# Where VectorE subtracts the transposed attention weights within a step, and where it splits the next weight tile

## The reference, cut to what matters

```python
z = jnp.einsum('bhqd,bhkd->bhqk', qb, kb).astype(jnp.float32) * scale
mask = s_idx < t_idx
log_one_minus = jnp.where(mask, jax.nn.log_sigmoid(-z), 0.0)
suffix = lax.cumsum(log_one_minus, axis=3, reverse=True) - log_one_minus
weights = jnp.where(mask, jnp.exp(jax.nn.log_sigmoid(z) + suffix), 0.0)
outs.append(jnp.einsum('bhqk,bhkd->bhqd', weights.astype(vb.dtype), vb))
...
y_sb = jnp.einsum('bsw,wd->bsd', (o_sb * jax.nn.silu(sb_z)).astype(x.dtype), w_o_sb[layer])
```

## Time and profile before

| | us |
|---|---|
| median of 3 runs | 809.22 |
| the profiled execution | 809.52 |
| its span, first to last instruction | 807.8 |
| TensorE matmuls busy in the span | 791.0 |
| TensorE weight loads busy | 662.3 |
| VectorE busy | 581.6 |
| ScalarE busy | 410.0 |
| granted TensorE clock | 0.999 of full speed |

### The profile page before, as it was taken

How to read it: one execution, slowest core, us unless ns; L and a number is a source line. 1 busy time by engine, 2 the same in 40 slices (tenths; PEclk the granted TensorE clock), 3 DMA queues, 4 the chain that set the end, 5 groups by cost and what they waited for, 6 DMA issues and landing times.

```text
span 807.8 us, 11845 instructions
## 1 busy us (share of the span) xinstructions
PE 791.0 (98%) x4441; PEld 662.3 (82%) x4441; DVE 581.6 (72%) x823; ACT 410.0 (51%) x706; POOL 30.4 (4%) x32
## 2 busy tenths in 40 slices
PE   5999999999999999999999999999999999999996
PEld 4778888888888888889889888888888888888885
DVE  6528997989798798956645646566457777779985
ACT  7526675666666466655244144244343343365442
POOL 1540000000000000020000000000000000000000
PEclk9999999999999999999999999999999999999999
DMA  9862112202120220021111010244443333395222
GB/s 316 277 225 53 27 28 52 52 26 52 53 51 26 53 52 27 27 80 54 30 50 27 3 52 27 79 143 152 147 131 105 105 104 105 105 360 213 105 105 104
DMA packets 72483, 76.31 MB, mean 94 GB/s; under 512 B 3804, under 2 KB 57207, under 8 KB 71928
## 3 DMA queue, kind: packets, MB, share of 16 engines
q1 hardware_dynamic: 72386, 75.71, 29.5%
q10 hardware_dynamic: 54, 0.01, 0.0%
HBM read 55.79 MB, written 15.73 MB: 89 GB/s over the span
## 4 chain that ended last, share of the span: by engine, by line
PE 94%; ACT 2%; DVE 1%; DMA 1%; issue 1%; SPq 0%; DVEq 0%; ACTq 0%
PE pj L698 29%; PE tr L1002 5%; PE sc L950 5%; PE ob L950 5%; PE ob L790 5%; PE pj L842 4%; PE ob L1002 4%; PE pj L1002 4%; PE tr L800 4%; PE sc L1002 3%; PE pj L714 3%; PE pj L823 3%; PE tr L1060 2%; PE sc L767 2%; PE sc L766 2%; PE pj L1060 2%
## 5 line engine op out<-in xcount | busy, mean ns | idle before, releaser
L698 PE MATMUL pj<-h_hi,w_lo 128*128 128x512 f32 x336 | 134.2, 399 | 0.0
L698 PE MATMUL pj<-h_hi,w_hi 128*128 128x512 f32 x336 | 133.9, 398 | 0.0
L698 PE MATMUL pj<-h_lo,w_hi 128*128 128x512 f32 x336 | 133.8, 398 | 0.0
L1671 DVE TENSOR_TENSOR_SCAN surv<-surv 128x128 f32<-128x128 f32 (+3 forms) x64 | 86.5, 1351 | 16.3 <-ACT beta L1169 15.9
L698 PEld LDWEIGHTS pj<-h_hi,w_lo 128*128 128x128 f32 x336 | 63.5, 189 | 12.1 <-issue 0.5
L698 PEld LDWEIGHTS pj<-h_lo,w_hi 128*128 128x128 f32 x336 | 63.3, 189 | 12.0 <-issue 0.3
L698 PEld LDWEIGHTS pj<-h_hi,w_hi 128*128 128x128 f32 x336 | 63.6, 189 | 11.6 <-issue 0.2
L1210 ACT ACTIVATE wt_hi<-tr 128x512 fp32r<-128x512 f32 (+2 forms) x96 | 43.6, 490 | 37.8 <-PE tr L800 36.3
L1594 DVE TENSOR_TENSOR w_lo<-w_raw,w_hi 128x1024 fp32r<-128x1024 f32 x33 | 40.3, 1222 | 27.0 <-ACT w_hi L1102 26.7
L1703 DVE TENSOR_TENSOR wt_lo<-tr,wt_hi 128x512 fp32r<-128x512 f32 (+2 forms) x96 | 50.2, 550 | 7.9 <-ACT wt_hi L1210 7.4
L1674 DVE TENSOR_TENSOR beta<-beta,surv 128x128 f32<-128x128 f32 (+3 forms) x64 | 48.6, 759 | 2.2
(11 more groups left out here) (400 smaller groups left out, 1910.3 us busy)
## 6 DMA issues: line engine op xcount, KB each, us to landing
w_raw<-in_w_in SPq DMA_DIRECT2D x30, 512.0 KB, 3.8
y_scratch<-y_ring SPq DMA_DIRECT2D x28, 256.0 KB, 2.0
graw<-in_w_in SPq DMA_DIRECT2D x14, 512.0 KB, 5.2
y_back<-y_scratch SPq DMA_DIRECT2D x14, 512.0 KB, 5.2
x_t<-in_x SPq DMA_DIRECT2D x8, 512.0 KB, 6.6
wrow<-in_w_out SPq DMA_DIRECT2D x4, 1024.0 KB, 7.2
w_scratch<-wsum SPq DMA_DIRECT2D x4, 1024.0 KB, 5.0
wout_raw<-in_w_out SPq DMA_DIRECT2D x8, 512.0 KB, 7.2
```

Of the source, the lines that this page charges most:

```text
L698: mm = pe.matmul(pj[bank][:, :], (w_lo if p == 2 else w_hi)[:, slot, k, :], (h_lo if p == 1 else h_hi)[:, k, HALF * h:HALF * h + HALF], st ...
L1671: dve.tensor_tensor_scan(s[:, ::-1], s[:, ::-1], s[:, ::-1], 1.0, ALU.mult, ALU.bypass)\
```

## The change

Three statements of the VectorE list of a step trade places; no instruction is added, removed or altered, and no other engine's list changes.

```diff
@@ -1690,20 +1690,12 @@
                         if k < KT - 1 or p < 2:
                             continue
                         c = 8 * i + 6 + 2 * j + h
+                        if h == 0:
+                            low_part(4 * i + 4 + j, j % 2)
                         if j == 0:
                             dve.wait_ge(proj_act, c + 1)
                             dve.tensor_tensor(z_silu[:, HALF * h:HALF * h + HALF], pj[h][:, :], z_sig[:, :],
                                               ALU.mult).then_inc(proj_free, 1)
-                    for n, r in enumerate(ROUNDS):
-                        if r[0] == "w" and r[1] == step:
...
-                            dve.wait_ge(tr_act, RPP * i + R0 + n + 1)
-                            dve.tensor_tensor(wt_lo[g % 2][:, b0:b0 + nb, qs],
...
                     if step >= 3 and step % 2:
...
-                    for j, h, k, p in plan[step]:
-                        if (h, k, p) == (0, KT - 1, 2):
-                            low_part(4 * i + 4 + j, j % 2)
+                    for n, r in enumerate(ROUNDS):
+                        if r[0] == "w" and r[1] == step:
...
+                            dve.wait_ge(tr_act, RPP * i + R0 + n + 1)
+                            dve.tensor_tensor(wt_lo[g % 2][:, b0:b0 + nb, qs],
```

More of the change, by code:

```diff
@@ L1696, in pair @@
                                               ALU.mult).then_inc(proj_free, 1)
-                    for n, r in enumerate(ROUNDS):
-                        if r[0] == "w" and r[1] == step:
-                            unit, b0, nb = r[2:]
-                            g = unit % 8 // 2
-                            qs = slice(P * (unit % 2), P * (unit % 2) + P)
-                            dve.wait_ge(tr_act, RPP * i + R0 + n + 1)
-                            dve.tensor_tensor(wt_lo[g % 2][:, b0:b0 + nb, qs],
-                                              tr[n % 2][:, 0:P * nb].rearrange("p (b q) -> p b q", q=P),
-                                              wt_hi[g % 2][:, b0:b0 + nb, qs].bitcast(F32),
-                                              ALU.subtract).then_inc(tr_free, 1)
                     if step >= 3 and step % 2:
@@ L1717, in pair @@
                                           low, z_silu[own, 256 * g:256 * g + 256], ALU.mult).then_inc(g_done, 1)
-                    for j, h, k, p in plan[step]:
-                        if (h, k, p) == (0, KT - 1, 2):
-                            low_part(4 * i + 4 + j, j % 2)
+                    for n, r in enumerate(ROUNDS):
+                        if r[0] == "w" and r[1] == step:
+                            unit, b0, nb = r[2:]
+                            g = unit % 8 // 2
+                            qs = slice(P * (unit % 2), P * (unit % 2) + P)
+                            dve.wait_ge(tr_act, RPP * i + R0 + n + 1)
+                            dve.tensor_tensor(wt_lo[g % 2][:, b0:b0 + nb, qs],
+                                              tr[n % 2][:, 0:P * nb].rearrange("p (b q) -> p b q", q=P),
+                                              wt_hi[g % 2][:, b0:b0 + nb, qs].bitcast(F32),
+                                              ALU.subtract).then_inc(tr_free, 1)
             with dve.Fori(0, PAIRS - 1) as i:
```

## The result

The changed kernel takes 814.26 us (median of 4, 813.72 to 814.44) against 809.37 of the kernel before: ratio 1.0064, 95% interval 1.0052 to 1.0077. It is slower by 4.9 us; the forecast was 814.3, in a range of 811.9 to 817.0. In a second comparison it was 814.44 against 809.31, ratio 1.0068 (1.0055 to 1.0082).

A forecast was written before the change was run, and what follows sets the result against it. TensorE was taken as the bound, its matmuls busy 791.0 of 807.8 us. +1.31 us in each of the first three pairs (3.9) and 1.0 in the last make +4.9: forecast 814.3 us, range 811.9 to 817.0.

The forecast's parts named there:

- Who waits for `wt_lo`: Second pair: TensorE's AV products and transpositions wait for the delayed `wt_lo`; VectorE's sum of work per step stays the same.
- five partial sums: TensorE's lateness: 0.4 us at AV(7), 0.89 at step 9's scores, 0.69 after AV(9), 0.38 after AV(13), 1.31 behind T(16).
- The loss at AV(7): Step 7: AV(7) reads the later `wt_lo`(6) and loses some 0.4 us, not added because the next wait swallows it.
- What is won back at AV(9) and AV(13): Old waits vanish because TensorE comes later: 0.2 us at AV(9), 0.31 at AV(13).
- rival B: Moved work fills VectorE's waits for ScalarE; AV(9) and AV(13) stop waiting, T(8) and T(16) don't stall: 807.5 us, chance 0.05.
- The stall at T(16): Steps 15 to 16: both moves delay `wt_lo`(15); next product starts at 202.38, +1.31 us in all, 0.93 of it new stall.
- the slot of `low_part` ahead of `o_low`: Step 15: time `low_part` takes on VectorE before `o_low` and `G`, put at 1.15 us.
- 0.66 us in hand: Step 16: slack T(16) was said to have over the end of `wt_lo`(15), counted from its start at 200.28.
- A: Only one of the two stalls comes, since ScalarE or VectorE runs ahead: about 0.6 us per pair, 812.0; chance 0.09.
- C: Nothing moves: T's bank is free for another reason, or stalls and recovered waits cancel: 809.5 us; chance 0.07 with D.
- D: The lists on the chip don't follow the diff, called hardly possible; chance 0.07 with C.
- shorten the restart: Weight loads done inside a TensorE stall would make its restart cheaper, about 0.2 us per stall, as in the small bound.

The follow-up runs named there:

- the earlier split: Kernel before the change, with weight tiles 1 and 2 split (`high_part` on ScalarE, `low_part` on VectorE) in steps 5 and 10 instead of 6 and 11: 807.18 against 809.31 us.
- The kernels that keep one alone: T(8): changed kernel, old order in step 15, 810.33 us, likewise only `o_low` and `G` moved; T(16): changed kernel, `wt_lo` first in step 7, 812.08; against 808.96.

## Why the prediction was right

**Who waits for `wt_lo`: shown.** The forecast followed TensorE's readers of `wt_lo` one by one, and the table above has each of its five partial sums within 0.03 us, but for the last, which is 0.11 off. That VectorE's own total is unchanged and beside the point is shown by its 63.11 us and by the scan of step 8.

**The loss at AV(7) is swallowed by T(8): shown.** TensorE is 0.42 late behind AV(7) and 0.91 behind T(8), as with `o_low` and `G` alone, where AV(7) lost nothing (0.89). The moment at which `wt_lo`(7) ends is set by VectorE's list and did not depend on when TensorE arrived, so the two waits make a maximum here and not a sum.

**What is won back at AV(9) and AV(13): shown.** 0.21 and 0.31 in every version in which T(8) stalls. For AV(9) the reason given holds. For AV(13) the number is right and the reason incomplete. The prediction gives one reason why VectorE reaches `wt_lo`(12) about when it did: the work is the same in another order. It does end at about its old place in the pair, 53.18 us into it instead of 53.04, but two things make that up. The scan of step 11 waits for ScalarE, which follows TensorE, and so starts 0.70 later (45.64 instead of 44.94):

```profile
178.53 1.23 DVE L1671 TENSOR_TENSOR_SCAN surv<-surv 128x512 f32<-128x512 f32 x1 [0.81 <-ACT beta L1169]
...
185.39 0.68 DVE L1716 TENSOR_TENSOR wt_lo<-tr,wt_hi 128x512 fp32r<-128x512 f32 x1
```

From its start to the end of `wt_lo`(12) it takes 7.54 us instead of 8.10, because what now stands ahead of `wt_lo`(11) fills the 0.46 in which `wt_lo`(11) waited for ScalarE. With `o_low` and `G` alone in front it is 7.54 as well, with `low_part` alone in front (in steps 1, 11 and 15) 7.56. Without that filling `wt_lo`(12) would, as an estimate from these numbers, end at 45.64 + 8.10 = 53.74, behind the 53.59 at which AV(13) would be due (185.02 - 132.12 + 0.69), and AV(13) would have gone on waiting; the prediction names this filling in its rival B and not in its own sum.

**The stall at T(16), where both moves meet: shown, and forecast a tenth too small.** Either move alone is covered (0.36 and -0.18 at the product behind T(16), the shifts that TensorE brought with it), both together cost 1.03 more. The forecast said 0.93. The term that was mis-sized is the slot of `low_part` ahead of `o_low`: 200.62 - 199.37 = 1.25 us instead of 1.15. It could have been read from the earlier trace rows: in step 15 `o_low` started 0.03 after the end of `wt_lo` (199.65 against 199.62), while in step 7 it started 0.09 before it (167.64 against 167.73). The "0.66 us in hand" beside the sum is too small as well, it should be 0.99, but the sum does not use it: it goes from the end of `wt_lo`(15) to the product. In the last pair the loss up to AV(17) was 1.09, where I took 1.0. From the trace the four pairs make 3 times 1.43 and 1.09, 5.4 us, the timed runs 4.9 and 5.1 (ratios of 1.0064 and 1.0068 are 5.2 and 5.5). So the pairs cost about 0.5 more than the +4.9 of the forecast, and that the median of 814.26 falls on the forecast of 814.3 is in part luck. In the two profiled executions the difference is 4.0 and not 5.4: the stretch ahead of the pairs is 0.7 shorter in the one of after (58.31 against 58.99 us), and so is the one far behind them that is named in the section on the result.

**The rivals.** B had the right ingredient, VectorE filling its waits for ScalarE, and the runs with `low_part` alone and with the earlier split show it as a gain of 0.2 to 0.6 per pair; its condition, that T(8) and T(16) have enough in hand, fails in the change. A, that only one stall comes, is out: both are in the trace. The kernels that keep one alone cost +1.4 us (T(8)) and +3.1 (T(16)). C and D, no change, are out by the +4.9. The Trainium skill (TensorE: Matmul & The Clock Gate, Architectural detail: the array is 16× 32×32) says that TensorE's queue can pull weight loads ahead of matmuls in flight; the prediction weighed whether that would shorten the restart. No run here shows a load pulled past a transposition that waits: the loads of T(16) begin at 202.38 after a wait of 1.23 us, and the first load behind them only at 203.23. The restart cost 0.47 behind `wt_lo`(15), against 0.46 behind `wt_lo`(7) before.

## What to carry to other kernels

When instructions of one engine trade places, its total does not change and its busy share tells nothing; list who waits for the one that moved back, and hold the length of what now stands ahead of it against the time that each reader has in hand. Two moves that are each covered can together exceed the cover: here 1.25 and 1.01 us ahead of the same operation. Of their 2.26 us VectorE's own idle time took 0.22 (`wt_lo`(15) ends 3.33 us after the multiplication instead of 1.29), the reader had 0.99 in hand, and the remaining 1.05 is the loss (measured: 1.03). Count what a reader has in hand up to the first thing that really comes late, here the product behind T(16) and not the start of T(16). And put work that nobody awaits where its engine already waits (here one step earlier), not behind or ahead of what somebody does.

## What the hardware showed besides

In the rows shown an instruction on VectorE mostly starts 0.07 to 0.1 us before the end of the one ahead of it. `o_low` on the upper 64 partitions (reading `ob` in the lower 64), and what follows `G` there, starts 0.03 after it instead, in each kernel: 199.65 against an end at 199.62 before, 200.62 against 200.59 after. In step 7, on the lower partitions, the overlap is there. A multiplication behind its scan has no overlap either, wherever it stands (178.32 against an end at 178.29 before). No run here took apart whether the partitions, or what else, are the cause.
